# Windowed attention beside a projection: scores of two heads from both partition halves, one shift instruction, and two copies in another order

## The reference

```python
def _dilated_attention(q, k, v, slopes):      # C_CONFIGS = ((128, 1), (512, 4), (2048, 16)); C_DH = 64
    for g, (window, dil) in enumerate(C_CONFIGS):
        offs = dil * jnp.arange(-per_side, per_side + 1)
        s = jnp.einsum('bqhd,bqjhd->bhqj', q_blk[:, :, g], k_sel) * scale
        s = s - slopes[g][:, None, None] * jnp.abs(offs).astype(F32)
        s = jnp.where(valid, s, MASK_VALUE)
        ...
    w = jax.nn.softmax(jnp.stack(lses), axis=0)      # the three groups share one softmax

# reference(), odd layer
z = h @ odd_w_in[o_i]                                # 1024 -> 5120 columns
o_c = _dilated_attention(q_c, k_c, v_c, slopes)      # slopes: 2 ** (-8 n / 24), n = 1..24, as (3 groups, 8 heads)
o_d = _multiscale_pool(z[..., n_c:], pool_w[o_i], pool_scale[o_i])
mixed = jnp.concatenate([o_c, o_d], axis=-1) @ odd_w_out[o_i]
x = x + g1 * mixed
```

## Time and profile before

| | |
|---|---|
| median of 3 runs | 857.54 us (856.28 to 860.87) |
| the profiled execution, its own time | 856.18 us |
| its span (first to last instruction) | 854.5 us |
| mean granted clock of TensorE | 0.942 |
| PE busy | 779.9 us (91% of the span) |
| DVE busy | 596.3 us (70%) |
| ACT busy | 423.7 us (50%) |
| chain that ended last | PE 81%, DVE 12%, DMA 3% |

### The profile page before, as it was taken

One profiled execution on the slowest core, in us unless ns is written; L12 is line 12 of the kernel. 1 busy time (PEld: TensorE's weight loads), 2 busy tenths in 40 slices (PEclk: granted clock), 3 DMA queues, 4 the chain that ended last, 5 costly groups with the idle time before them and its releaser, 6 DMA issues.

```text
span 854.5 us, 16791 instructions
## 1 busy us (share of the span) xinstructions
PE 779.9 (91%) x6581; PEld 737.9 (86%) x6581; DVE 596.3 (70%) x856; ACT 423.7 (50%) x665; POOL 64.9 (8%) x72
## 2 busy tenths in 40 slices
PE   3399998985897999999997999999797999999996
PEld 3299986675797999999997999998687999999995
DVE  3976686779857999975447678866446788886444
ACT  4344465331335666665334555545345666666322
POOL 0200116000200000000000004400000000000000
PEclk9799998568899999999999999999898999999998
DMA  9999876321363999855761997665113778865501
GB/s 360 346 265 333 298 264 228 99 75 41 94 195 100 292 291 290 254 196 198 267 224 51 290 340 254 226 199 172 50 50 100 197 221 239 242 222 206 194 2 50
DMA packets 160053, 171.24 MB, mean 200 GB/s; under 512 B 5179, under 2 KB 142340, under 8 KB 158980
## 3 DMA queue, kind: packets, MB, share of 16 engines
q1 hardware_dynamic: 153667, 147.50, 54.6%
q0 software_dynamic: 6336, 23.07, 7.5%
HBM read 169.50 MB, written 1.05 MB: 200 GB/s over the span
## 4 chain that ended last, share of the span: by engine, by line
PE 81%; DVE 12%; DMA 3%; issue 2%; ACT 2%; SPq 1%; DVEq 0%; POOLq 0%; ACTq 0%
PE acc L1130 54%; PE big L1130 14%; DMA ada_raw<-in_ada_w 2%; DVE mod_acc L827 2%; DVE qk L310 2%; PE aux L1190 2%; PE big L1289 1%; PE acc L1294 1%; DVE w_lo L758 1%; PE big L1404 1%; DVE mod_acc L768 1%; DVE work L801 1%; DVE rstd L789 1%; PE aux L1200 1%; DVE o_rms L970 1%
## 5 line engine op out<-in xcount | busy, mean ns | idle before, releaser
L1130 PE MATMUL acc<-h_hi,w_hi 128*128 128x256 f32 x1248 | 353.2, 283 | 17.7 <-DVE h_lo L808 14.8
L1130 PE MATMUL acc<-h_lo,w_hi 128*128 128x256 f32 x1248 | 349.6, 280 | 0.0
L1130 PE MATMUL acc<-h_hi,w_lo 128*128 128x256 f32 x1248 | 349.6, 280 | 0.0
L758 DVE TENSOR_TENSOR w_lo<-w_raw,w_hi 128x1024 fp32r<-128x1024 f32 x220 | 266.6, 1237 | 117.2 <-ACT w_hi L503 117.1
L503 ACT ACTIVATE w_hi<-w_raw 128x1024 fp32r<-128x1024 f32 x220 | 224.6, 1050 | 94.1 <-PE big L1130 62.4
L1130 PEld LDWEIGHTS acc<-h_hi,w_hi 128*128 128x128 f32 x1248 | 239.4, 192 | 20.1 <-issue 18.1
L1130 PEld LDWEIGHTS acc<-h_lo,w_hi 128*128 128x128 f32 x1248 | 238.9, 191 | 0.3
L1130 PEld LDWEIGHTS acc<-h_hi,w_lo 128*128 128x128 f32 x1248 | 238.9, 191 | 0.0
L1130 PE MATMUL big<-hid_hi,w_hi 128*128 (+1 forms) x352 | 97.5, 277 | 0.0
L1130 PE MATMUL big<-hid_lo,w_hi 128*128 (+1 forms) x352 | 97.2, 276 | 0.0
L1130 PE MATMUL big<-hid_hi,w_lo 128*128 (+1 forms) x352 | 97.2, 276 | 0.0
(11 more groups left out here) (193 smaller groups left out, 918.3 us busy)
## 6 DMA issues: line engine op xcount, KB each, us to landing
w_raw<-in_ffn_w_up SPq DMA_DIRECT2D x88, 512.0 KB, 5.0
ada_raw<-in_ada_w POOLq DMA_DIRECT2D x44, 512.0 KB, 5.6
w_raw<-in_ffn_w_down SPq DMA_DIRECT2D x44, 512.0 KB, 4.0
w_raw<-in_odd_w_in SPq DMA_DIRECT2D x40, 512.0 KB, 5.4
w_raw<-in_even_w_in SPq DMA_DIRECT2D x32, 512.0 KB, 6.0
ada_raw<-in_ada_w SPq DMA_DIRECT2D x30, 512.0 KB, 3.9
ada_first<-in_ada_w SPq DMA_DIRECT2D x5, 1024.0 KB, 8.2
w_raw<-in_even_w_out SPq DMA_DIRECT2D x8, 512.0 KB, 5.1
```

The source lines that it names most:

```text
L758: dve.tensor_tensor(w_lo[:, n % SPLIT, part], w_raw[:, n % RAW, part], w_hi[:, n % SPLIT, part].bitcast(F32), ALU.subtract).then_inc(s_lo, 1)
L1130: ins = pe.matmul(dst, lhsT, rhs, start=start and n == 0, stop=stop and n == 2, skip_group_check=True)
```

## The change

The three groups' slopes stand in a fixed ratio for every head: slope(g, h) = slope(0, h) * 2^(-8g/3). The constant table of distances now carries this factor, and the 16 columns of slopes are gone; the shift is one instruction over 384 columns in place of three over 256, 64 and 64. At even steps PE computes the scores of steps s and s+1, with the products of the two heads in alternation, into both banks; at odd steps it computes none. The wait ahead of them is for the shift of step s-1. The split of OO+1 leaves the turn of p = 19 and stands behind step 11 on ACT and DVE; ACT's copy of `h_hi` channels 4 to 7 moves ahead of its step 11.

```diff
@@ shape_constants
-        a[:, C_DIST + t * ROW:C_DIST + (t + 1) * ROW] = np.where(ok, off, BIG)
-    for h in range(C_HEADS):
-        a[:, C_SLOPE + 2 * h] = np.where(half, -slope(2, h), -slope(1, h))
-        a[:, C_SLOPE + 2 * h + 1] = np.where(half, -slope(1, h), -slope(2, h))
+        a[:, C_DIST + t * ROW:C_DIST + (t + 1) * ROW] = np.where(ok, off * 2.0 ** (-8.0 * group / C_GROUPS), BIG)
@@ ACT
-                split_hi(0, n + SPLIT)
+                if p < N_OI - 1:
+                    split_hi(0, n + SPLIT)
             act.wait_ge(pool_taken, 4)
+            nc.scalar.activation(h_hi[:, 4:8, :], work[:, 4:8, :], ACT.Copy).then_inc(h_hi_ready, 1)
             for s in range(BESIDE_ENDS, STEPS + 4):
                 dilated(s)
                 if s == BESIDE_ENDS:
-                    nc.scalar.activation(h_hi[:, 4:8, :], work[:, 4:8, :], ACT.Copy).then_inc(h_hi_ready, 1)
+                    split_hi(0, OO + 1)
@@ DVE
-                for at0, at1, k in ((0, T, -slope(0, h)),
-                                    (T, T + 64, consts[:, C_SLOPE + 2 * h:C_SLOPE + 2 * h + 1]),
-                                    (T + 64, ROW, consts[:, C_SLOPE + 2 * h + 1:C_SLOPE + 2 * h + 2])):
-                    col = C_DIST + t * ROW
-                    ins = dve.scalar_tensor_tensor(out=cs[s % 4][:, at0:at1], in0=consts[:, col + at0:col + at1],
-                                                   scalar=k, in1=big[:, s % 2, at0:at1], op0=ALU.mult, op1=ALU.add)
-                return ins
+                col = C_DIST + t * ROW
+                return dve.scalar_tensor_tensor(out=cs[s % 4], in0=consts[:, col:col + ROW], scalar=-slope(0, h),
+                                                in1=big[:, s % 2, 0:ROW], op0=ALU.mult, op1=ALU.add)
-                if p >= FIRST_HEADS:
+                if FIRST_HEADS <= p < N_OI - 1:
                     split_lo(0, OI + p + SPLIT)
             for s in range(BESIDE_ENDS, STEPS + 3):
                 dilated(s)
                 if s == BESIDE_ENDS:
                     mixed_lo(MIX_AT[1] + 1, slice(4, 8))
+                    split_lo(0, OO + 1)
@@ PE
-            def dil_scores(bank, h, t):
-                lane = slice((h % 2) * DH, (h % 2 + 1) * DH)
+            def dil_scores(h, t):
+                lanes = (slice(0, DH), slice(DH, 2 * DH))
...
+                for b in (0, 1):
+                    pe.matmul(big[:, b, 0:T], rows(lanes[b], 0, 0, t * P, P), rows(lanes[b], 6, 0, 0, T), start=True, stop=True)
                 for side in (0, 1):
                     tok0 = t * P + 64 * side
                     for block, g in enumerate((1, 2) if side == 0 else (2, 1)):
                         at0 = T + 64 * block
-                        ins = pe.matmul(bank[64 * side:64 * side + 64, at0:at0 + 64], rows(0, g, tok0, 64),
-                                        rows(6, g, tok0, 64), start=True, stop=True, skip_group_check=True)
+                        for b in (0, 1):
+                            ins = pe.matmul(big[64 * side:64 * side + 64, b, at0:at0 + 64], rows(lanes[b], 0, g, tok0, 64),
+                                            rows(lanes[b], 6, g, tok0, 64), start=True, stop=True, skip_group_check=True)
@@ PE dilated
-                if s < STEPS:
+                if s < STEPS and s % 2 == 0:
...
                     if s >= 2:
-                        pe.wait_ge(shifted, base + s - 1)
-                    dil_scores(big[:, s % 2, :], 2 * (s // 4) + s % 2, s // 2 % 2).then_inc(scored, 1)
+                        pe.wait_ge(shifted, base + s)
+                    dil_scores(2 * (s // 4), s // 2 % 2).then_inc(scored, 2)
```

More of the change, by code:

```diff
@@ L74 @@
 C_DIST = C_FLIP + P
-C_SLOPE = C_DIST + TT * ROW
-C_INV = C_SLOPE + 2 * C_HEADS
+C_INV = C_DIST + TT * ROW
 C_ALL = C_INV + 4 * T
@@ L1397, in _, with rows @@
             mod_turn(2, 16, aux[:, 1])
-            def dil_scores(bank, h, t):
-                lane = slice((h % 2) * DH, (h % 2 + 1) * DH)
-                def rows(first, g, tok0, tokens):
+            def dil_scores(h, t):
+                lanes = (slice(0, DH), slice(DH, 2 * DH))
+                def rows(lane, first, g, tok0, tokens):
                     f = g * 4 + h // 2
                     return zo[lane, first + f // 2, (f % 2) * T + tok0:(f % 2) * T + tok0 + tokens]
-                pe.matmul(bank[:, 0:T], rows(0, 0, t * P, P), rows(6, 0, 0, T), start=True, stop=True)
+                for b in (0, 1):
+                    pe.matmul(big[:, b, 0:T], rows(lanes[b], 0, 0, t * P, P), rows(lanes[b], 6, 0, 0, T), start=True, stop=True)
                 for side in (0, 1):
```

## The result

The changed kernel is slower, by 0.7%. Its median is 866.47 us (863.53 to 870.62, 20 runs), that of the kernel before 859.44 us (854.23 to 869.93, 20 runs); the ratio is 1.0068 [1.0045, 1.0091]. The forecast was 846. The profiled execution took 867.73 us with a span of 866.1, against 856.18 and 854.5.

What follows compares the result with a forecast made beforehand. PE bounds steps 0 to 10 beside the projection; behind 594 us lie about 7 us of holes and low clock. 3.8 (five pairs) + 6.9 (tail) + 0.6 (overlap) = 11.3 us off 856.2: 844.9, median 846; range 842 to 852.

Steps and rivals of the forecast that it cites:

- The shorter table changes nothing in time: Constant table of distances without its slope columns: no effect on time, since it is read once, long before.
- behind `mod_sum`: After the attention's tail: nothing is touched and the weights are already waiting for PE, so the gain is kept; change 0.
- The slower case that I named: Score pairs: every turn between the array's halves drains it; at 0.20 us a turn 4.8 us lost, 862; chance 0.05.
- up to the last unit's eviction, after its stall: Beside the projection: five pairs save 0.75 us each, 3.8 in all; the last unit ends 0.6 later with overlap.
- stall in the last unit: Unit 19, steps 9 and 10: PE must wait 1.3 us for DVE's shift of step 9 and its maximum.
- tail, eviction to `mod_sum`: From the projection's last eviction to `mod_sum`'s first product: 18.5 us instead of 26.3, holes and low clock gone.
- wait for the eviction: Tail behind unit 19: PE's values of step 8 wait for the eviction, about 1.1 us, replacing the two old holes.
- stall at step 10's values: Tail: PE's values of step 10 wait about 0.6 us for DVE, which is late after the split of OO+1.
- The pair: Scores of two heads together on PE: 1.67 us per insertion against 2.42 for two single ones, 0.75 saved.
- The rival of full overlap: Score pairs: the array's two halves run fully side by side, 14.9 us gained, 842.5; chance 0.08.
- DVE itself has 24 us of idle: Attention beside the projection: DVE, idle 24 of 94 us and getting lighter, would not hold up PE's pairs.
- The shift: DVE, each step: three instructions become one of 0.55 us, 0.25 less; hidden before 594, counted in the tail's steps 12 to 15.

Runs made afterwards that it cites:

- e1: The changed kernel with 16 unused columns put back into the constant table, so every tensor behind it has its address of before; 845.67 us, 0.988 of the kernel before.
- e2: The kernel before with only the slope columns gone, the shift still three instructions, PE's and ACT's order that of before; 876.87 us, ratio 1.024.
- e5: The kernel before, addresses kept, with only PE's part of the change: scores of two heads at even steps; 853.07 us, ratio 0.994.
- e6: The kernel before with the order alone: OO+1 split behind step 11, copy of h_hi channels 4 to 7 ahead of it; 850.04 us, ratio 0.992.
- e7: The kernel before with the single shift instruction alone, table padded so all addresses are those of before; 859.44 us, ratio 1.003.

## Why the prediction was wrong

**The step that failed** is one sentence: "The shorter table changes nothing in time: it is read once, long before." The table's size is also an offset. It moved `h` and `hid` against `w`, and 5,280 projection matmuls became some 5 ns longer (mean at full clock 119.1 against 114.0 ns): about 27 us (the spans of the changed kernel and of e1 differ by 24.4), of which 12.2 and 10.1 lie outside the attention. e2, which takes out the columns and leaves PE's work, the count of shift instructions and the order as they were, is 2.4% slower than the kernel before; e1, which puts them back, takes 845.67 us. This was not among the rivals, and the reason given for keeping the gain ("behind `mod_sum` nothing is touched") rests on the same omission. The range was built from the attention only. The slower case that I named, turns that drain the array, had nothing to do with the slowdown.

**The terms of the sum**, on e1 against the kernel before:

| term | forecast, us | e1 |
|---|---|---|
| up to the last unit's eviction, after its stall | 3.8 - 0.6 = 3.2 | 3.3 (3.4 from step 0 on) |
| stall in the last unit | 1.3 | 1.1 |
| tail, eviction to `mod_sum` | 26.3 to 18.5 (18.1 with the overlap in its two pairs) | 26.3 to 18.0 |
| wait for the eviction | 1.1 | 1.1 |
| stall at step 10's values | 0.6 | 0.6 |
| behind `mod_sum` | 0 | 1.2 less |
| median | 846 | 845.67 |

So the steps on stalls, order and clock were right where the addresses were held. That the first row agrees is chance: a pair gave more than forecast, and most of the surplus was lost in one unit, as told below. The 1.2 us behind `mod_sum` are no effect of the change that I can name; single units there ran at 117.8 ns in one profile and at 113.3 in the other. The chain of the tail could be played through from rows, including what is late next: e5 and e6 show that the order carries it, and that the pair's wait (3.6 us in e5) is harmless only because the order was changed with it.

**The pair** was mis-sized: I took 0.75 us saved and it is 1.2 (2.42 to some 1.23 with the way in and out; the blocks themselves 1.02 and 1.03). The rival of full overlap, given 0.08 because "the two instructions of a product come one after the other on the same half", was right. The Trainium skill, "TensorE: Matmul & The Clock Gate", Part 3, says that products on different row groups run concurrently; with 1.03 us for ten products against 1.02 for five this case agrees. That five pairs then gave 3.4 us from step 0 on, and not 5.9 - 1.2 = 4.7, has another cause. One unit, from step 3 to step 4, takes 6.20 us in e1 where it took 5.43. PE's wait in it (528 to 545 us), and what DVE and POOL did (start, us):

```profile
PE acc L1127 <- DVE w_lo L758: 0.4, 1, 0.4
```

```profile
529.90 2.40 POOL L475 TENSOR_TENSOR s<-s 128x807 f32<-128x807 f32 x1
531.23 4.16 DVE L758 TENSOR_TENSOR w_lo<-w_raw,w_hi 128x1024 fp32r<-128x1024 f32 x2 [0.33 <-ACT w_hi L501]
```

Beside the pooling on POOL the split takes DVE 4.16 us for two halves (3.91 in the kernel before) and 2.35 two units later. It comes too late for a PE whose blocks got shorter: two starts of PE lie 0.66 us apart there, in place of 0.11. Before, the longer score blocks covered it. That it is the pooling which makes the split longer is argued from their lying side by side; no run moved it away. "DVE itself has 24 us of idle" was an average over 94 us and hid this one unit. The remaining 0.5 us are spread over the other units, 0.2 of them in the next one.

**The shift**: forecast as nothing before 594 and a little in the tail; 0.547 us an instruction as estimated, and e7 finds nothing measurable. It is possible that its 0.5 us are there: the interval reaches 0.1% below 1.

## What to carry to other kernels

Whoever changes a tensor's size moves everything placed behind it; compare the number of matmuls in equal stretches far from the edit before explaining anything near it, and pad the freed columns back in as the first experiment. When a freed resource makes room on one engine, play the chain on through the engine that becomes late next, and change order and batching together: the batch of two heads waits for a shift that only the new order makes early. Products with a contraction of 64 on the two partition halves, alternated into different banks, cost PE here what one half's cost (1.03 against 1.02 us a block).

## What the hardware showed that I had not expected

- Two operands of a matmul interact by their start addresses. With float32r operands of 128x128 and 128x256, the pace is mostly 113.3 ns at a distance of -64 bytes modulo 256 (streamed minus stationary), mostly 117.8 at +64, and 117.3 to 120.0 at 0, +96, -128, -96 and -32. The Trainium skill, "TensorE: Matmul & The Clock Gate", Part 2 (Step-by-step: what each phase is for), has it that loading the next weights does not steal read bandwidth from the running matmul; no run here separates the two reads, but where the two operands lie changes the pace by up to 6%. The cause inside the chip stays open: nothing in a trace shows it. Distances that are no multiple of 32 bytes were not tried.
- Even at the good distance there are two paces, 113.3 and 117.8 ns (as there are 118.7 and 120.0 in the changed kernel), and in the profiles here a long stretch keeps the one that it starts in. In e5's profiled execution (863.57 us, where its median is 853.07) PE began 172 matmuls in 20 us of the down projection, which is the slower one:

```profile
60.00:80.00 20.00, 20.00 (x178) 20.00 (x178) 13.89 (x12) 8.86 (x11) 1.58 (x3) 1.00 1.05 334
...
400.00:420.00 20.00, 20.00 (x172) 20.00 (x172) 9.44 (x8) 7.22 (x8) 0.00 (x0) 1.00 0.52 186
```

This fits the spread of the kernel before (854 to 870 us in 20 runs) and the narrower one of the kernel after (864 to 871), which has no fast pace to fall out of; with one profile a kernel, that is argued and not shown. What decides the pace at a stretch's start is open too.
- The low clock of the tail follows the holes: with them closed (e6) it is granted in full from 594 to 622 us, with them somewhat shorter (e7) `half_of(0)` still ran at 1.2 GHz and took 5.46 us.
